# Streaming encoder kernel: gate's weight sums on GpSimd, the middle norm's squares regrouped, the first `down` add two operations earlier

## The reference

```python
def _swiglu(x, w_gate, w_up, w_down):
    return (jax.nn.silu(x @ w_gate) * (x @ w_up)) @ w_down

x = x + 0.5 * _swiglu(_rmsnorm(x, ffn1_norm), ffn1_w_gate, ffn1_w_up, ffn1_w_down)
y, ... = _mixer(_rmsnorm(x, mix_norm), ...)   # gated convolution and mLSTM
x = x + y
x = x + 0.5 * _swiglu(_rmsnorm(x, ffn2_norm), ffn2_w_gate, ffn2_w_up, ffn2_w_down)
return _rmsnorm(x, final_norm), ...
```

## Time and profile before

| | |
|---|---|
| median of three runs | 1870.73 us (1869.62 to 1872.44) |
| profiled execution | 1873.01 us, its span 1871.3 us |
| TensorE busy | 1829.0 us, 98% |
| VectorE / ScalarE / GpSimd busy | 69% / 40% / 9% |
| mean granted clock of TensorE | 0.993 |

### The profile page before, as it was taken

The page is one execution under the profiler, slowest core; times in us unless marked ns, Lnnn a source line. Parts: engine busy times, 40 slices in busy tenths (PEclk is TensorE's granted clock), DMA queues, the critical chain, the costliest instruction groups (busy, mean ns, idle before and its releaser), DMA issues.

```text
span 1871.3 us, 32710 instructions
## 1 busy us (share of the span) xinstructions
PE 1829.0 (98%) x12145; PEld 1799.2 (96%) x12145; DVE 1292.9 (69%) x2168; ACT 745.9 (40%) x1227; POOL 164.8 (9%) x220
## 2 busy tenths in 40 slices
PE   8999999999999978999999999999999999999998
PEld 8999999999999978999999999999999999999998
DVE  6578788888665555612588867567888888755565
ACT  5344334444333343333344534233433344333343
POOL 1610000000000032200000013610000000000001
PEclk9999999999999989999999999999999999999999
DMA  6222222423445444211111331123322223354554
GB/s 206 69 68 68 90 67 71 108 67 90 113 140 151 135 113 150 71 46 45 35 35 34 127 108 32 37 68 86 95 67 86 71 67 94 101 154 134 148 145 137
DMA packets 242049, 174.51 MB, mean 93 GB/s; under 512 B 8488, under 2 KB 228472, under 8 KB 241976
## 3 DMA queue, kind: packets, MB, share of 16 engines
q1 hardware_dynamic: 241888, 173.49, 32.3%
q10 hardware_dynamic: 88, 0.02, 0.0%
HBM read 164.56 MB, written 8.92 MB: 93 GB/s over the span
## 4 chain that ended last, share of the span: by engine, by line
PE 44%; DVE 10%; DMA 3%; issue 2%; ACT 2%; SPq 0%; DVEq 0%; POOL 0%; ACTq 0%
PE bank L224 14%; PE bank L229 13%; PE bank L230 13%; DMA raw<-in_ffn_w_gate 2%; DVE ffn_t L739 2%; DVE ffn_w_lo_more L300 1%; DVE ffn_hidden L839 1%; DVE ffn_t_work L734 1%; DVE ffn_hidden_lo L873 1%; DVE x L754 1%; PE bank L228 1%; ACT w_hi L294 0%; PE bank L2734 0%; DMA raw<-in_ffn_w_up 0%; PE bank L2748 0%
## 5 line engine op out<-in xcount | busy, mean ns | idle before, releaser
L224 PE MATMUL bank<-in_hi,w_hi 128*128 128x352 f32 x1536 | 488.8, 318 | 3.8 <-DVE w_lo L1738 1.6
L229 PE MATMUL bank<-in_lo,w_hi 128*128 128x352 f32 x1536 | 480.6, 313 | 0.0
L230 PE MATMUL bank<-in_hi,w_lo 128*128 128x352 f32 x1536 | 480.5, 313 | 0.0
L224 PE MATMUL bank<-ffn_hidden_hi,ffn_w_hi_more 128*128 128x352 f32 x1056 | 336.9, 319 | 10.7 <-ACT ffn_hidden_hi L537 6.2
L754 DVE SCALAR_TENSOR_TENSOR x<-bank,x 128x352 f32<-128x352 f32 x528 | 253.0, 520 | 82.8 <-PE bank L228 45.7
L224 PEld LDWEIGHTS bank<-in_hi,w_hi 128*128 128x128 f32 x1536 | 290.7, 189 | 8.0 <-issue 2.5
L229 PEld LDWEIGHTS bank<-in_lo,w_hi 128*128 128x128 f32 x1536 | 290.8, 189 | 1.2
L230 PEld LDWEIGHTS bank<-in_hi,w_lo 128*128 128x128 f32 x1536 | 290.7, 189 | 0.0
L229 PE MATMUL bank<-ffn_hidden_lo,ffn_w_hi_more 128*128 128x352 f32 x924 | 290.4, 314 | 0.0
L230 PE MATMUL bank<-ffn_hidden_hi,ffn_w_lo_more 128*128 128x352 f32 x924 | 290.2, 314 | 0.0
L300 DVE TENSOR_TENSOR w_lo<-raw,w_hi 128x1024 fp32r<-128x1024 f32 x132 | 164.7, 1253 | 112.0 <-ACT w_hi L294 111.7
(11 more groups left out here) (293 smaller groups left out, 3288.9 us busy)
## 6 DMA issues: line engine op xcount, KB each, us to landing
raw<-in_ffn_w_gate SPq DMA_DIRECT2D x88, 512.0 KB, 5.0
raw<-in_ffn_w_down SPq DMA_DIRECT2D x84, 512.0 KB, 4.2
raw<-in_ffn_w_up SPq DMA_DIRECT2D x44, 512.0 KB, 6.4
ffn_raw_more<-in_ffn_w_up SPq DMA_DIRECT2D x44, 512.0 KB, 6.9
raw<-in_w_in SPq DMA_DIRECT2D x24, 512.0 KB, 4.0
x_parked<-x SPq DMA_DIRECT2D x3, 1408.0 KB, 9.1
x<-x_parked SPq DMA_DIRECT2D x3, 1408.0 KB, 10.0
raw<-in_w_out SPq DMA_DIRECT2D x8, 512.0 KB, 3.7
```

Source lines behind the costliest of these rows:

```text
L224: pe.matmul(out, w_hi, in_hi, start=first, stop=False)
L229: pe.matmul(out, w_hi, in_lo, start=False, stop=False)
L230: return pe.matmul(out, w_lo, in_hi, start=False, stop=last)
```

## The change

1. `t_make` for gate leaves VectorE's program and stands in GpSimd's, behind the activation sums: once for pair 2, then in a loop for pairs 3 to 10, always in the order 0, 2, 1, 3. Up's stay on VectorE. GpSimd waits for both gate loads, then for the same t_low counts as before.
2. In the seven-product pairs the first residual add stands before the product of hidden tile 3, two operations earlier; the second right behind that product; the third and fourth behind low half 3.
3. In `alone` with the norm of block 0: four squares before the silu of hidden tile 0, the other four behind the next pair's first highs. The eight squares of block 1 go into the split of block 0, one before each high. The next pair's two `down` highs go into the split too, at k = 4. On VectorE adds 4 to 7 go between the first steps of the split (k = 1 to 4).

```diff
@@ -466,6 +466,10 @@
         if following:
             following.loads(sp)
 
+    def t_parts(i):
+        hi, lo = t_halves(i)
+        return sh.t_work[:, 1 if i == 2 else 0, :], hi, lo
+
 
     @block.gpsimd
     def _(pool):
@@ -501,6 +505,25 @@
             step_op(third, f0, third, ALU.subtract)
             whole(f3, inputs["x12"][k])
             step_op(f3, f3, f2, ALU.subtract)
+        def t_make(w, i, kind, pair):
+            w11, w21 = (sh.raw[SLOT[w, 0]][:, h * 512:(h + 1) * 512] for h in range(2))
+            w12, w22 = (sh.raw[SLOT[w, 1]][:, h * 512:(h + 1) * 512] for h in range(2))
+            work = t_parts(i)[0]
+            if i == 0:
+                for j in range(2):
+                    pool.wait_ge(f.loaded[w][j], pair * 16 + (base * 16 + 16))
+            a, c = {0: (w12, w11), 1: (w22, work), 2: (w22, w12), 3: (w21, work)}[i]
+            if i == 2:
+                pool.wait_ge(q.t_low, kind * 4 + (T_SPLIT[2] - 4)) if not (isinstance(kind, int) and kind == 0) else None
+            elif not (isinstance(kind, int) and kind == 0 and i == 0):
+                pool.wait_ge(q.t_low, kind * 4 + {0: 0, 1: T_SPLIT[0], 3: T_SPLIT[1]}[i])
+            pool.tensor_tensor(work, a, c, ALU.subtract).then_inc(q.t_made, 1)
+
+        for i in (0, 2, 1, 3):
+            t_make("gate", i, 0, PLAIN)
+        with pool.Fori(PLAIN, PAIRS_F - 1) as pair:
+            for i in (0, 2, 1, 3):
+                t_make("gate", i, kind_index(pair, "gate") + 2, pair + 1)
         if following:
             for b in range(BLOCKS):
                 if b == 2:
@@ -508,10 +531,6 @@
                 norm_add(pool, sh, NORM_MIX + b)
         if tail:
             tail.pool(pool)
-
-    def t_parts(i):
-        hi, lo = t_halves(i)
-        return sh.t_work[:, 1 if i == 2 else 0, :], hi, lo
 
 
     @block.scalar
@@ -676,7 +695,11 @@
             number, n = pair + PAIRS_F, pair
             step = (n * 2 + rounds * 2, n * 2 + (LATER_PASSES * 4 + rounds * 2),
                     n * 8 + (LATER_PASSES * 16 + rounds * 8))
-            highs("down", number, (s.down_done, step[2]))
+            if not (head and isinstance(pair, int) and pair > PAIRS_F - 3):
+                highs("down", number, (s.down_done, step[2]))
+            if norm == NORM_MIX:
+                for k in range(4):
+                    norm_square(act, sh, norm, k)
 
             def next_highs():
                 if not last:
@@ -691,10 +714,10 @@
                 tail.act_round(act, tiles, hidden_of, next_highs)
             else:
                 hidden_of(0, None)
-                if norm is not None:
-                    for k in range(KT):
+                next_highs()
+                if norm == NORM_MIX:
+                    for k in range(4, KT):
                         norm_square(act, sh, norm, k)
-                next_highs()
                 if last and head:
                     act.wait_ge(s.up_done, step[0] + 1)
                     following.early_high(act)
@@ -704,7 +727,13 @@
                 weight_high(act, sh, f, "gate", 1, number + 1)
                 weight_high(act, sh, f, "up", 1, number + 1)
             if norm is not None:
-                norm_split_act(act, sh, norm)
+                def between(k):
+                    if norm == NORM_MIX:
+                        norm_square(act, sh, norm + 1, k)
+                    if k == 4:
+                        highs("down", number + 1, (s.down_done, step[2] + 8))
+
+                norm_split_act(act, sh, norm, between)
             if last and head:
                 act.wait_ge(s.up_done, step[0] + 2)
                 following.late_high(act)
@@ -795,10 +824,6 @@
                 if last_of_pair:
                     weight_low(dve, sh, f, "gate", 0, pair + 1)
                     weight_low(dve, sh, f, "up", 0, pair + 1)
-                if last_of_pair and pair == 1:
-                    dve.wait_ge(f.loaded["gate"][1], (PLAIN + base) * 16 + 16)
-                    t_make("gate", 0, 0)
-                    t_make("gate", 2, 0)
                 if last_of_pair:
                     for k in sums_of(pair, b, "middle"):
                         s_lows(k)
@@ -815,13 +840,11 @@
                 if last_of_pair and pair == 0:
                     weight_low(dve, sh, f, "up", 1, pair + 1)
                 if last_of_pair and pair == 1:
-                    t_make("gate", 1, 0)
                     t_low(2, 0)
                 for d in range(4, 6):
                     add(r * 8, b, d, down_bank)
                 if last_of_pair and pair == 1:
                     t_low(1, 0)
-                    t_make("gate", 3, 0)
                 for d in range(6, KT):
                     add(r * 8, b, d, down_bank)
                 for k in sums_of(pair, b, "end"):
@@ -944,9 +967,6 @@
                     norm_split_dve(dve, sh, own_norm, gain, between, lambda: adds(range(14, 16)))
                 up_lows(pair + 1)
             else:
-                if not last:
-                    t_make("gate", 0, ku + 1)
-                    t_make("gate", 2, ku + 1)
                 both22("up", ku, hidden)
                 hidden_make(0)
                 if not last:
@@ -958,19 +978,16 @@
                 c21("up", ku, hidden)
                 hidden_make(2)
                 low(1)
-                if not last:
-                    t_make("gate", 1, ku + 1)
                 low(2)
                 c12("up", ku, hidden)
+                own_adds_done(count)
+                adds(range(1))
                 hidden_make(3)
+                adds(range(1, 2))
                 if not last:
                     t_low(1, ku + 1)
-                own_adds_done(count)
-                adds(range(1))
                 low(3)
-                adds(range(1, 4))
-                if not last:
-                    t_make("gate", 3, ku + 1)
+                adds(range(2, 4))
                 adds(range(4, 16))
                 if last:
                     up_lows(pair + 1)
@@ -1008,12 +1025,14 @@
                 norm_roots_dve(dve, sh, norm, gate_bank[0])
             if not last:
                 weight_low(dve, sh, f, "up", 1, number + 1)
-            for d in range(4, KT):
-                add(count, 2, d, down_bank)
-                if last and head and d == 5:
-                    following.late_low(dve)
             if norm is not None:
-                norm_split_dve(dve, sh, norm, V_MIX)
+                norm_split_dve(dve, sh, norm, V_MIX,
+                               lambda k: add(count, 2, 3 + k, down_bank) if 1 <= k <= 4 else None)
+            else:
+                for d in range(4, KT):
+                    add(count, 2, d, down_bank)
+                    if last and head and d == 5:
+                        following.late_low(dve)
             if last and head:
                 norm_means_dve(dve, sh, NORM_MIX + 2, gate_bank[0])
 
```

## The result

The changed kernel takes 1878.86 us (median of five runs, 1877.24 to 1881.03) against 1870.73 (1869.62 to 1872.44) for the kernel before. The ratio is 1.0036, interval 1.0025 to 1.0047: slower by a little more than can be told from no change. The forecast was 1876 and slower. By the ratio that is 6.7 us, by the two medians 8.1, where the sum had 5.4. The profiled execution has a span of 1876.7 us, and that is 5.4 above the profiled one of before. That the spans agree to the tenth is luck; that the change costs 5 to 9 us is not.

The account below looks back on a forecast made before the run. TensorE, working 98% of the span, bounds the kernel, so only its waits can be gained. Loops +1.3, entries +0.7 and middle norm +3.4 sum to +5.4 us: 1876 us from a median of 1870.73, range 1863 to 1882.

Parts of the forecast that it names:

- Gate's subtractions: Loop pairs: 1.27 us each on GpSimd, blocking VectorE; TensorE waits 0.81 in place of 0.72, loops +1.3 us.
- The forecast chain: Loop pair from 1376: GpSimd's subtractions hold VectorE's product and low, so the third hidden product ends at 1401.63.
- The moved add: Loop pairs: the add ends 0.7 us ahead of need, but a wait for the hidden halves replaces its wait; neutral.
- Entries: First loop pair of each half: +1.0 us in the first, -0.3 in the second, together +0.7 us.
- Block 0's squares: Middle norm: squares 4 to 7 wait for the up load; TensorE's 2.6 us wait grows 2.4, first add 1.9 later.
- The split: Middle norm: block 0's split beside GpSimd's additions takes 9.7 + 3.9 = 13.6 us.
- The end of pair 9: Long wait moves from column sums to second half of `down`; hidden's high half ready at 706.0, +3.4 us.
- the next three at half pace cost 0.6: Pair 9, after the long wait: the three adds following the first cost 0.6 us at half clock.
- The faster one: VectorE and GpSimd don't block each other: loops gain 6.6 us, norm 0.5, entries 1; 1863 us, chance 0.20.
- The one within 0.2%: Norm costs 3.4 us, but GpSimd's chain meets idle VectorE and each loop pair gains 0.2; 1872 us, chance 0.27.

Follow-up runs that it names:

- e2: The kernel before with the middle norm's part of the change alone; 1879.70 us, ratio 1.0034 to the kernel before.
- e5: e2 with each of GpSimd's seven additions of block 1's squares replaced by three memsets, that sum left out; 1876.17 us, ratio 1.0015.
- e6: e2 with block 0's squares 4 to 7 put back ahead of the weights' highs on ScalarE; 1870.91 us, ratio 0.9990.
- e7: e1 with each of GpSimd's gate subtractions replaced by two memsets and two one-element subtractions; 1865.77 us, ratio 0.9960.
- e3: The kernel before with the residual adds moved as in part 2 and nothing else; 1866.07 us, ratio 0.9963.
- e11: The whole changed kernel with block 0's squares 4 to 7 put back ahead of the weights' highs; 1872.79 us, ratio 1.0000.
- e4: e1 with the moved add taken back, so only gate's subtractions go to GpSimd; 1895.53 us, ratio 1.0126.
- e9: e8 with block 1's column sums behind the fifth down product, hidden's second half ahead of the next weights; 1848.92 us, ratio 0.9877.
- e10: The kernel before with the moved add and e6's norm, VectorE keeping gate's subtractions; 1862.84 us, ratio 0.9949.
- e1: The changed kernel with the middle norm put back: gate's subtractions on GpSimd and the moved add stay; 1874.70 us, ratio 1.0009.
- e8: e3 with another middle norm: squares rearranged, none of GpSimd beside the split, next down weights inside it; 1857.24 us, ratio 0.9909.

## Why the prediction was right, and where its steps were not

**Gate's subtractions.** Right. Alone they take 1.28 us (1.27 forecast), 1.35 in the mean of 36 with the ones that had to wait. The forecast chain holds almost to the operation: first product and low half locked, the third hidden product ends at 1406.64, less the shift of 5.14 that is 1401.5 (1401.63 forecast), and TensorE stops in front of the thirteenth `down` matmul and at the low half behind it. It stops for 0.5 us, where 0.81 was forecast, and the loops come out at +0.8 and +0.8, 0.11 a pair, for a forecast of 0.09. That close a match is more than the traces can tell: in e2, e5 and e6, whose loops are those of the kernel before, the same two stretches come out between -0.2 and +0.7. On the rule of the Trainium skill (SBUF — State Buffer, "Who interferes with whom") the traces agree in both directions: reads shut a two-input VectorE operation out (1.33 us for 0.52), and memsets, which only write, don't (0.52 in e7).

**The moved add.** Wrong, and hidden by the sum. The prediction said that "the moved add by itself is neutral: what it was late for has another cause next". The next cause is not the add's: it is GpSimd's shut-out, and without it nothing takes the wait's place. e3 gains 7 us. The loops are near zero because 4.3 us gained and 5.9 lost by another part meet there (7 and 8.6 by the ratios). I had followed one chain with both edits in it and priced the pair rightly; I had not priced either alone.

**Entries.** Not settled: +1.0 and -0.3 were forecast. The shift is 0.08 at 150, and it falls by 0.66 between 1250 and 1290. But e2, e5 and e6, which have both entries as before, are at -1.5, -0.5 and -0.5 at 150, and between 1250 and 1290 at -0.4, -0.2 and +0.1, so one execution can't tell these terms from nothing.

**Block 0's squares.** Right: the up load's landing holds squares 4 to 7, the wait is 5.6 for 2.6 (+2.4 forecast, +3.0 measured), and the first add comes 2.5 later in its own time where 1.9 stood. e6 and e11 show that this is the step that decides whether the whole change costs anything. What the sum had too low is what followed from it.

**The split.** Right in kind and size: 14.0 us for 13.6, and e5 shows 3.4 of it to be the shut-out (3.9 forecast).

**The end of pair 9.** The long wait moved where it was said to, 7.3 us, ending at 709.22; less the 2.45 us by which this kernel was already behind, that is 706.8 for 706.0. The term that failed is "the next three at half pace cost 0.6": the spreading of the roots stands behind the fifth down product, and the clock until then is 0.50 from 709 to 712 and 0.79 to 716, so that from the first add (+3.9 then) to the split 1.6 were lost. The split of block 1 begins at 716.71 for 708.79 with its adds in both, 5.5 later in its own time, where +3.4 was summed. At 737 4.85 is left of it, where the sum had 3.4. The norm part alone has 6.4 by the ratio.

**What made up for it.** Two amounts that the sum did not have: the mixer gave back 1.6 us at 877 (e2, e4, e6, e9, e10 and e11 have the same step, e1, e3, e5, e7 and e8 don't), and 1.5 went at 503 to 515 to a later up load, as in eight of the other eleven profiled executions. These come and go between kernels; what decides them is not settled by these runs.

**The rivals.** The faster one, no shut-out, is refuted as a description by the held operations and by e7 and e5. Its prices were too good as well: with no wait for the add the loops gain 4.3 us in e3 and 4.8 in e7, not 6.6; and with none of GpSimd's reads beside the split the norm part still loses (e5: ratio 1.0015, +2.9 us between 661 and 737) where the prediction had a gain of 0.5, the bound of its own sum. The one within 0.2% needed GpSimd to land in VectorE's idle moments; it does so in its fourth subtraction only.

## What to carry to other kernels

Price the parts of a change one by one even if they meet in the same stretch: here 5.9 us lost and 4.3 gained stood in the same loops, and one order of two lines was worth 7 to 8. Before work is given to GpSimd, look at which VectorE operations with two SBUF inputs run at that moment, and who waits for them; the busy time saved says nothing. Work that needs no load does not go behind work that waits for one on an engine that works in order, and weights for the next stage may be split before, not after, a long run of elementwise work, so that the loads behind them can leave: e8 and e9 do so, though not that alone.

## What the runs showed of the hardware

A GpSimd operation with a single SBUF input is held as well: the copy of block 0's first square, at 655.11 in the changed kernel, takes 1.15 us beside VectorE's weight lows (from 653.45, two in 2.47), for 0.48. The `scalar_tensor_tensor` of the split, two SBUF inputs, is held like a `tensor_tensor` (1.31 and 1.25 for 0.58). A held VectorE operation ended 0.38 us after GpSimd's both times in the pair above, though it takes 0.52 alone. The product and the low half cost 0.81 and 0.87 us more by it; together that is about what VectorE sheds ahead of the third hidden half, three subtractions of 0.6.
